# A two-block network on one core: the split of the output projections' input, a norm's sum and the attention's waits are moved

## The chip, the core and the metric

The kernel runs on one core of a Trainium2 chip. The metric is the device time in microseconds (us) of one execution. The engines are named as in the profile: PE is TensorE (PEld its weight loads), DVE is VectorE, ACT is ScalarE, POOL is GpSimd, and SP issues most of the DMAs.

## What is computed

The input is one sequence of 512 tokens with 1024 features, in float32. It goes through two different networks, one after the other. Cut to what matters here:

```
# first block (one layer)
h = rms_norm(x) ; four branches: rwkv7, mamba2 (state space), rg-lru, retention
y_ssd = rms_norm(y_state_space, norm_w)                  # a norm of its own over the 1024 features
merged = sum over the branches m of sigmoid(h @ gate_m) * (y_m @ w_branch_m)
x = x + merged @ w_out ; x = x + conv_ffn(rms_norm(x))

# second block (two layers)
h   = rmsnorm(x) ; z = h @ w_in
o_a = nsa attention, o_b = sliding window attention with sinks
o_c = mla attention: q = rmsnorm(cq) @ w_q_up, kv = rmsnorm(ckv) @ w_kv_up, 8 heads, causal softmax
g_a, g_b, g_c = sigmoid(h @ w_branch_gate)
merged = g_a * (o_a @ w_a) + g_b * (o_b @ w_b) + g_c * (o_c @ w_c)
x = x + merged @ w_out ; x = x + ffn(rmsnorm(x)) ; x = x + gated per-layer embedding
```

## The kernel before, in words

Everything stays in SBUF with features on the partitions: an activation of 1024 features is eight tiles of 128x512. The weights stream in from HBM, one tile after the other in the order in which PE uses them.

**Products.** Each float32 product is made from three fp32r products. A number is split into a high part (a copy by ACT) and a low part (number minus high part, by DVE), and PE computes high x high, low x high and high x low (`proj`, L603, whose three matmuls are L612, L613 and L614). An output tile over 1024 input features is 8 such triples, 24 matmuls (`tile`, L617). Before each triple k PE waits for the low part of input tile k. Each weight tile is split in the same way: `whi` by ACT (L1328) and `wlo` by DVE (L2044). Weights have three raw and three split buffers; the split of weight n is ordered on ACT and DVE at the place where weight n-3 is named (`ahead`, L247), and waits for PE to be done with weight n-3. Input splits are made by ACT copies and by `split_lo` (L2050, its subtraction is L2053). `h_of` gives the wait for a low part that is made by DVE, or by POOL for every third tile; `h_of_dve` the wait for one that DVE always makes.

**Order of the work.** There is one hand-written program per engine: all work of an engine is in the order of its program, and semaphores join them. `due` gives the waits that are still needed. PE writes to a ring of 7 PSUM banks (`bank`): taking a bank means waiting for whoever read its last content.

**The four merges of the first block** (`merge`, L854, L1521, L2362). For each of 8 output tiles PE computes a gate tile g(j) and a branch tile b(j), in the order g(0), g(1), b(0), g(2), b(1), and so on. In the merge of the state space branch (m = 0) the norm of that branch is applied late: ACT squares the 8 tiles (L1550), DVE adds them up (L2372), PE sums over the partitions with two float32 matmuls against ones (`total`, L1021, L1026), ACT takes the square root (L1338) and DVE the reciprocal (L2378) `MR`, by which the gates are multiplied. PE issues that sum right after b(0).

**Each layer of the second block** runs `z_proj`, `nsa`, `mla`, `branches`, the output projection (`out_proj` on ACT and DVE, `residual` on PE), `ffn` and `ple`. The two layers use different buffers: `Hx[0]` (HH, HL) and `Hx[1]` (HBh, HBl) hold the split normalized input of layer 0 and of layer 1.

- `attend` (L1162, L1860, L2893) interleaves the heads of an attention: a "first" step computes scores on PE (L1173), their maximum on DVE (L2901) and the exponential on ACT (L1868); a "second" step transposes (L1183); a "third" step multiplies by the values (L1192), with side work in between. `needs` of a job lists what the score step waits for, `vneeds` what the value step waits for.
- `mla`: PE computes q tiles and k tiles, ACT copies them out into per-head tiles QALL and KALL (L1928, L1929), two heads to a tile; DVE rotates part of q (`rope`, tile 4 for heads 0 to 3, tile 5 for heads 4 to 7). The 4 value tiles (L1269 to L1271) are side work of the first heads, and ACT copies them out into CV. Every score step waits for all of rope, all of k; every value step for all 4 tiles of CV.
- `branches` (L1279, L1966, L3027): for j in 0..7 and m in 0..2 PE computes a gate tile (24 matmuls) and a branch tile (12 matmuls). DVE multiplies the gate tile by the norm (L3051), ACT takes the sigmoid (L1978), DVE multiplies by the branch tile (L3038) and adds into the merged tile (L3043), which lies in MG in layer 0 and MGB in layer 1.
- `out_proj`: when all of `branches` is done, ACT copies the 8 merged tiles to `mp2` high parts (L1986); DVE makes the low parts of tiles 0, 1, 3, 4, 6 and 7, POOL those of 2 and 5 (`third_lo`, L3122). PE's output projection then uses them tile by tile.

What ACT and DVE do at the end of `branches` and after it, cut to its core:

```
# ACT, branches, for each j and m (n = 3 j + m)
hi(st, "g", j, m)                                  # splits one weight
wait gr(n) ; ACTV(tmp2[n % 4], tmp2[n % 4], ACT.Sigmoid)
hi(st, "b", j, m)
# ACT, out_proj
for j in range(8):
    ACTV(mp2[j][0], Mx[l][j], ACT.Copy)
```

Of the kernel before, what the change touches and what calls it, by code (L numbers as in the profile page):

```python
# [310 lines left out]
def build(nc, T, known=None):  # L311

    with ExitStack() as ctx:
# [100 lines left out]
        Mt = tiles(MG)  # L414
# [32 lines left out]
        with ExitStack() as c1:  # L447
# [43 lines left out]
            with ExitStack() as c2:  # L491
                tmp3, ACCt, tsq = tiles(sb(c2, "tmp3", 6 * S)), sb(c2, "ACCt", S), tiles(sb(c2, "tsq", 2 * S))
                with ExitStack() as c3:
                    mp2 = pairs(c3, "mp2", 8)
                act2 = pairs(c2, "act2", 11)
                PLE = sb(c2, "ple", 2 * S)
# [15 lines left out]
        TBx, OCx = [m[0:4] for m in Mx], [m[0:4] for m in Mx]  # L512
        ZCx = [m[4:8] + [ZC] for m in Mx]
# [40 lines left out]
        def nsa_jobs(l):  # L554
            jobs = []
            for qb in range(4):
# [3 lines left out]
                common = dict(qb=qb, qs=qs, needs=[("dve", "rope", "z%d" % l, 12)],  # L560
                              vneeds=[("dve", "vt", l, 3), ("act", "zt", l, 3)],
# [14 lines left out]
        def mla_jobs(l):  # L576
            st = "la%d" % l
            needs = [("dve", "rope", st, 5), ("act", "up", st, "k", 3), ("pool", "kpe", l)]
            return [dict(qb=qb, qs=slice(128 * qb, 128 * qb + 128), needs=needs, vneeds=[("act", "cv", st, 3)], pb=pbL, pt=ptL, key=("ml", l, qb),
                         nk=128 * (qb + 1), k0=0, mask=128, extra=0, s=smL[qb % 3], q=lambda h: QH[h], k=lambda h: KH[h],  # L580
                         v=lambda h, kb: CV[:, kb, 64 * h:64 * h + 64], beside=[] if qb else [(("vp", l), 5)], then=[(("out", l, qb, "c"), 3)])
                    for qb in range(4)]
# [12 lines left out]
        def tensor_program(pe):  # L595
# [25 lines left out]

            def h_of(tag):
                return lambda k: [lo_key(tag, k)]
# [230 lines left out]
            def merge(m):  # L854
# [3 lines left out]
                for j in range(8):  # L858
                    if j < 7 and (m != 3 or j):
                        gate_tile(m, j + 1)  # L860
                    tile((st, "b", j), "w_br", (m, j), 8, yp, h_of_dve(st))
                    if m == 0 and j == 0:
                        total(LN["mn"])
# [298 lines left out]
            def attend(l, jobs, side):  # L1162
                banks = {}
                for what, *x in attention_steps(jobs):
                    if what == "begin":
                        banks[x[0]["key"]] = bank("ob", *x[0]["key"], hold=True)
                    elif what == "first":
# [3 lines left out]
                        for s in due("pe", *job["needs"]):  # L1171
                            pe.wait_ge(*s)
# [69 lines left out]
            def mla(l):  # L1242
                st = "la%d" % l
                for g in (1, 0):
                    w = W.take((st, "q", g), "w_q", (l, g), 2)
                    for j in (4, 5, 3) if g else (0, 1, 2):
                        proj(bank(st, "q", j), (st, "q", j), w, cqpx[l], h_of("cq%d" % l), 128 * (j - 3 * g))
# [5 lines left out]
                for j in range(4):  # L1253
                    proj(bank(st, "k", j), (st, "k", j), w, ckp, h_of("ck%d" % l), 128 * j)
# [54 lines left out]
            for l in range(2):  # L1309
# [4 lines left out]
                residual("wo%d" % l, "w_o2", (l,), mp2, h_of("mp%d" % l))  # L1314
# [5 lines left out]
        def scalar_program(act):  # L1320
# [200 lines left out]
            def merge(m, before):  # L1521
# [24 lines left out]
                if m == 0:  # L1546
# [7 lines left out]
                    hi(st, "b", 0)  # L1554
                    evac(("ss", "mn", 0), MR, ACT.Sqrt, ("rt", "mn"), scale=1.0 / 1024, bias=EPSC)
# [410 lines left out]
            def branches(l):  # L1966
# [5 lines left out]
                for j in range(8):  # L1972
                    for m in range(3):
                        n = 3 * j + m
                        hi(st, "g", j, m)
                        for need in due("act", ("dve", "gr", st, n)):
# [5 lines left out]
            def out_proj(l):  # L1982
                for need in due("act", *ends("br%d" % l)):
                    act.wait_ge(*need)
                for j in range(8):
                    ACTV(mp2[j][0], Mx[l][j], ACT.Copy).then_inc(*up("act", "hi", "mp%d" % l, j))  # L1986
# [51 lines left out]
        def vector_program(dve):  # L2038
# [988 lines left out]
            def branches(l):  # L3027
# [17 lines left out]
                for j in range(8):  # L3045
                    for m in range(3):
                        n = 3 * j + m
                        lo(st, "g", j, m)
                        for need in due("dve", ("pe", st, "g", j, m), OWN):
# [7 lines left out]
            def out_proj(l):  # L3057
                for j in range(8):
                    if j % 3 != 2:
                        split_lo(Mx[l][j], mp2[j], ("act", "hi", "mp%d" % l, j), lo_key("mp%d" % l, j))  # L3060
# [55 lines left out]
        def gpsimd_program(pool):  # L3116
# [62 lines left out]
            for l in range(2):  # L3179
# [12 lines left out]
                third_lo("mp%d" % l, Mx[l], mp2)  # L3192
# [163 lines left out]
```

## Time and profile before

| | us |
|---|---|
| three runs | 3991.91, 3993.53, 3997.42 |
| median of the three | 3993.53 |
| the profiled execution | 3995.15 |
| span of the profile (first to last instruction) | 3993.3 |
| mean granted TensorE clock in the profile | 0.977 of full |

The page of the profile gives for each engine its busy time and its share of the span: PE 3773.1 (94%), DVE 2163.7 (54%), ACT 1497.0 (37%), POOL 104.9 (3%). How to read the views used below: the list of waits names who sat idle, on which line and tile, who released it, and for how long in total, how often, and the longest. A line of the timeline is: start, duration, engine, line and operation, output tile <- input tiles, shapes, count, and in brackets the idle time before it and who ended it. The windows view gives the busy time of engines in a stretch and the granted TensorE clock as a share of full speed.

### The profile page before, as it was taken

To read this page: it belongs to the slowest core of one execution; us is meant where nothing else is said; L and a number is where in the kernel's file an instruction comes from. 1 tells how busy PE (TensorE), PEld (TensorE's weight loads), DVE (VectorE), ACT (ScalarE), POOL (GpSimd) and SP (SyncE) were. 2 spreads that over 40 slices of the span, in tenths; PEclk is the share of its full clock that TensorE was granted. 3 is DMA by queue.
4 is the path that set the end of the run, shared out by engine and by line. 5 is a ranking of instruction groups with operands and counts; after the bars stand their busy time and mean duration, and the time that the engine had idled before them with its cause. 6 is when DMAs were issued, how large, how long until landed. Compare 5 with 4: busy or idle time off the path is not lost.

```text
span 3993.3 us, 52039 instructions
## 1 busy us (share of the span) xinstructions
PE 3773.1 (94%) x22082; PEld 3043.1 (76%) x22082; DVE 2163.7 (54%) x3219; ACT 1497.0 (37%) x2555; POOL 104.9 (3%) x132
## 2 busy tenths in 40 slices
PE   8888899799999999999999999999998999999998
PEld 6678588676876777877777887888777778878886
DVE  6844635656443566467565445434565554454345
ACT  5733324135322344343355323323434453232233
POOL 0022000100000000000001000000000010000000
PEclk9999999899999999999999999999999999999999
DMA  3100123022231222323200132232232002322322
GB/s 138 58 3 3 54 85 106 16 74 79 101 113 51 79 89 80 101 88 104 86 1 17 64 97 96 93 101 88 94 102 65 1 17 85 98 94 88 102 88 81
DMA packets 90956, 297.52 MB, mean 75 GB/s; under 512 B 10083, under 2 KB 12643, under 8 KB 90212
## 3 DMA queue, kind: packets, MB, share of 16 engines
q1 hardware_dynamic: 88848, 286.50, 21.8%
q10 hardware_dynamic: 1876, 7.71, 0.5%
q8 instruction: 173, 2.83, 0.3%
q14 instruction: 59, 0.48, 0.0%
HBM read 292.07 MB, written 2.10 MB: 74 GB/s over the span
## 4 chain that ended last, share of the span: by engine, by line
PE 81%; DVE 12%; ACT 5%; issue 1%; POOL 1%; DMA 0%; SPq 0%; DVEq 0%; ACTq 0%; POOLq 0%
PE ps L612 20%; PE ps L614 20%; PE ps L613 20%; PE ps L1173 3%; PE ps L1192 3%; DVE wlo L2044 2%; ACT whi L1328 2%; PE ps L1183 2%; DVE ftm L2060 1%; PE ps L754 1%; PE ps L638 1%; PE ps L747 1%; PE ps L759 1%; PE ps L640 1%; PE ps L639 1%
## 5 line engine op out<-in xcount | busy, mean ns | idle before, releaser
L2044 DVE TENSOR_TENSOR wlo<-wraw,whi 128x1024 fp32r<-128x1024 f32 (+5 forms) x603 | 664.0, 1103 | 1293.3 <-ACT whi L1328 1287.7
L1328 ACT ACTIVATE whi<-wraw 128x1024 fp32r<-128x1024 f32 (+5 forms) x603 | 578.1, 959 | 1302.7 <-PE ps L614 1220.0
L612 PE MATMUL ps<-HH,whi 128*128 128x512 f32 x1816 | 722.7, 398 | 9.2 <-DVE HL L2623 4.7
L614 PE MATMUL ps<-HH,wlo 128*128 128x512 f32 x1816 | 709.6, 391 | 0.0
L613 PE MATMUL ps<-HL,whi 128*128 128x512 f32 x1816 | 709.6, 391 | 0.0
L612 PEld LDWEIGHTS ps<-HH,whi 128*128 128x128 f32 x1816 | 343.0, 189 | 91.5 <-DVE HL L2623 8.1
L613 PEld LDWEIGHTS ps<-HL,whi 128*128 128x128 f32 x1816 | 342.8, 189 | 77.1 <-issue 6.3
L614 PEld LDWEIGHTS ps<-HH,wlo 128*128 128x128 f32 x1816 | 342.4, 189 | 72.4
L612 PE MATMUL ps<-HBh,whi 128*128 128x512 f32 x752 | 298.8, 397 | 6.8 <-DVE HBl L2623 6.3
L613 PE MATMUL ps<-HBl,whi 128*128 128x512 f32 x752 | 294.2, 391 | 0.0
L614 PE MATMUL ps<-HBh,wlo 128*128 128x512 f32 x752 | 294.2, 391 | 0.0
L612 PEld LDWEIGHTS ps<-HBh,whi 128*128 128x128 f32 x752 | 142.1, 189 | 41.0 <-DVE HBl L2623 8.8
L613 PEld LDWEIGHTS ps<-HBl,whi 128*128 128x128 f32 x752 | 142.1, 189 | 31.5 <-issue 2.0
L614 PEld LDWEIGHTS ps<-HBh,wlo 128*128 128x128 f32 x752 | 141.9, 189 | 30.3
L1173 PE MATMUL ps<-KPALL,ZT 128*128 128x256 f32 (+3 forms) x384 | 141.7, 455 | 22.7 <-DVE VT L2889 7.8
L612 PE MATMUL ps<-act2h,whi 128*128 128x512 f32 x384 | 152.4, 397 | 0.0
L613 PE MATMUL ps<-act2l,whi 128*128 128x512 f32 x384 | 152.2, 396 | 0.0
L614 PE MATMUL ps<-act2h,wlo 128*128 128x512 f32 x384 | 152.2, 396 | 0.0
L2901 DVE TENSOR_REDUCE sm<-ps 128x1 f32<-128x256 f32 (+3 forms) x192 | 87.1, 455 | 102.9 <-PE ps L1175 101.7
L612 PE MATMUL ps<-yph,whi 128*128 128x512 f32 x256 | 101.0, 394 | 3.5 <-DVE ypl L2053 3.5
L613 PE MATMUL ps<-ypl,whi 128*128 128x512 f32 x256 | 100.3, 392 | 0.0
L614 PE MATMUL ps<-yph,wlo 128*128 128x512 f32 x256 | 100.2, 391 | 0.0
(636 smaller groups left out, 6464.1 us busy)
## 6 DMA issues: line engine op xcount, KB each, us to landing
wraw<-in_w_ff SPq DMA_DIRECT2D x88, 512.0 KB, 3.5
wraw<-in_w_bg SPq DMA_DIRECT2D x48, 512.0 KB, 3.5
wraw<-in_ffn_up SPq DMA_DIRECT2D x44, 512.0 KB, 3.2
wraw<-in_w_z SPq DMA_DIRECT2D x36, 512.0 KB, 3.2
wraw<-in_w_gate SPq DMA_DIRECT2D x32, 512.0 KB, 3.2
wraw<-in_w_br SPq DMA_DIRECT2D x32, 512.0 KB, 3.2
wraw<-in_w_rw SPq DMA_DIRECT2D x26, 512.0 KB, 3.3
wraw<-in_w_mam SPq DMA_DIRECT2D x24, 512.0 KB, 3.2
```

What stands on the lines that cost most here:

```text
L612: MM(b[0:m, :], hi[:, k, c0:c0 + m], x[0], start=(start and k == 0), stop=False)
L613: MM(b[0:m, :], hi[:, k, c0:c0 + m], x[1], start=False, stop=False)
L614: ins = MM(b[0:m, :], lo[:, k, c0:c0 + m], x[0], start=False, stop=(stop and k == n - 1))
L638: MM(b[:, 0:cols], x[0][:, cs], hi[:, k, 0:cols], start=first, stop=False)
L639: MM(b[:, 0:cols], x[1][:, cs], hi[:, k, 0:cols], start=False, stop=False)
L640: ins = MM(b[:, 0:cols], x[0][:, cs], lo[:, k, 0:cols], start=False, stop=end)
L1173: MM(b[:, 0:nk], job["q"](h)[:, qs], job["k"](h)[:, k0:k0 + nk], start=True, stop=False)
L1183: ins = TR(b[:, 128 * kb:128 * kb + 128], job["pb"][i % 3][:, 128 * kb:128 * kb + 128], C("ident"))
L1192: ins = MM(ob[:, 64 * h:64 * h + 64], job["pt"][i % 3][:, 128 * kb:128 * kb + 128], job["v"](h, kb), start=(kb == 0), stop=(kb == nkb - 1))
L1328: ACTV(W.pair_of(n)[0], W.raw_of(n), ACT.Copy).then_inc(*up("act", "whi", n))
L2044: TT(l, W.raw_of(n), h.bitcast(F32), SUB).then_inc(*up("dve", "wlo", n))
L2901: RED(s[:, h:h + 1], PS.of("sc", *key)[:, 0:job["nk"]], AXX, ALU.max, negate=True).then_inc(*(up("dve") if x else up("dve", "mx", *key)))
```

## The change

It has three parts.

1. **Output projections of the second block.** The buffer `mp2` goes; the split merged tiles are written to the other layer's buffers (`mp2x = [Hx[1], Hx[0]]`). In `branches`, at output tile j >= 1, ACT copies merged tile j-1 after the weight split of gate (j, 1), and DVE makes its low part after the weight split of gate (j, 2). Only tile 7 is left for `out_proj`. POOL makes none of them.
2. **State space sum.** PE issues it after g(2), before b(1), where it came after b(0); ACT's weight split that belongs to g(2) is put ahead of the square root.
3. **Attention waits.** The score step of MLA waits for the rope tile, q tile and k tile of its own head, the value step for the value tiles up to its own token block; the value steps of the other attentions also name only their own token block. `h_of` goes; the two uses in `mla` named DVE for tiles 0 and 1 already.

```
@@ buffers
-                with ExitStack() as c3:
-                    mp2 = pairs(c3, "mp2", 8)
+        mp2x = [Hx[1], Hx[0]]
@@ nsa_jobs
-                common = dict(qb=qb, qs=qs, needs=[("dve", "rope", "z%d" % l, 12)],
-                              vneeds=[("dve", "vt", l, 3), ("act", "zt", l, 3)],
+                common = dict(qb=qb, qs=qs, needs=lambda h: [("dve", "rope", "z%d" % l, 12)],
+                              vneeds=[("dve", "vt", l, qb), ("act", "zt", l, qb)],
@@ mla_jobs
-            needs = [("dve", "rope", st, 5), ("act", "up", st, "k", 3), ("pool", "kpe", l)]
+            def needs(h):
+                return [("dve", "rope", st, 4 + h // 4), ("act", "up", st, "q", h // 2), ("act", "up", st, "k", h // 2),
+                        ("pool", "kpe", l)]
-            ... vneeds=[("act", "cv", st, 3)] ...
+            ... vneeds=[("act", "cv", st, qb)] ...
@@ PE, merge
+                    if m == 0 and j == 1:
+                        total(LN["mn"])
                     tile((st, "b", j), "w_br", (m, j), 8, yp, h_of_dve(st))
-                    if m == 0 and j == 0:
-                        total(LN["mn"])
@@ PE, attend
-                        for s in due("pe", *job["needs"]):
+                        for s in due("pe", *job["needs"](h)):
@@ PE, program
-                residual("wo%d" % l, "w_o2", (l,), mp2, h_of("mp%d" % l))
+                residual("wo%d" % l, "w_o2", (l,), mp2x[l], h_of_dve("mp%d" % l))
@@ ACT, merge, m == 0
                     hi(st, "b", 0)
+                    hi(st, "g", 2)
                     evac(("ss", "mn", 0), MR, ACT.Sqrt, ("rt", "mn"), scale=1.0 / 1024, bias=EPSC)
@@ ACT, branches
                         hi(st, "g", j, m)
+                        if j and m == 1:
+                            for need in due("act", ("dve", "mt", st, 3 * j - 1)):
+                                act.wait_ge(*need)
+                            ACTV(mp2x[l][j - 1][0], Mx[l][j - 1], ACT.Copy).then_inc(*up("act", "hi", "mp%d" % l, j - 1))
@@ ACT, out_proj
-                for need in due("act", *ends("br%d" % l)):
-                    act.wait_ge(*need)
-                for j in range(8):
-                    ACTV(mp2[j][0], Mx[l][j], ACT.Copy).then_inc(*up("act", "hi", "mp%d" % l, j))
+                for need in due("act", ("dve", "mt", "br%d" % l, 23)):
+                    act.wait_ge(*need)
+                ACTV(mp2x[l][7][0], Mx[l][7], ACT.Copy).then_inc(*up("act", "hi", "mp%d" % l, 7))
@@ DVE, branches
                         lo(st, "g", j, m)
+                        if j and m == 2:
+                            split_lo(Mt[j - 1], mp2x[l][j - 1], ("act", "hi", "mp%d" % l, j - 1), ("dve", "lo", "mp%d" % l, j - 1))
@@ DVE, out_proj
-                for j in range(8):
-                    if j % 3 != 2:
-                        split_lo(Mx[l][j], mp2[j], ("act", "hi", "mp%d" % l, j), lo_key("mp%d" % l, j))
+                split_lo(Mx[l][7], mp2x[l][7], ("act", "hi", "mp%d" % l, 7), ("dve", "lo", "mp%d" % l, 7))
@@ POOL
-                third_lo("mp%d" % l, Mx[l], mp2)
```

## Rows read from the trace of the kernel before

**Rows 1.** PE's waits: line, releaser, total us, times, longest us.

```profile
PE ps L612 <- DVE mp2l L2053: 12.8, 2, 6.4
...
PE ps L1173 <- DVE VT L2889: 7.8, 2, 3.9
...
PE ps L1026 <- DVE msq L2372: 5.1, 1, 5.1
...
PE ps L1192 <- ACT CV L1338: 2.8, 2, 1.4
```

**Rows 2.** Windows, most of layer 0's branches: us, PE, PEld, DVE, ACT, POOL, clock, DMA.

```profile
2205.00:2421.00 216.00, 214.43 (x974) 175.37 (x973) 102.08 (x133) 68.70 (x105) 0.00 (x0) 0.99 0.27 87
```

**Rows 3.** Timeline of PE around the state space sum.

```profile
821.85 0.39 PE L614 MATMUL ps<-yph,wlo 128*128 128x512 f32 x1
827.38 2.08 PE L1026 MATMUL ps<-msq,CT 128*128 128x512 f32 x2 [5.14 <-DVE msq L2372]
...
835.33 0.39 PE L612 MATMUL ps<-yph,whi 128*128 128x512 f32 x1
```

**Rows 4.** Timeline of PE: such a sum at full clock, at another norm.

```profile
2480.77 1.02 PE L1026 MATMUL ps<-ACCt,CT 128*128 128x512 f32 x2
```

**Rows 5.** Timeline of DVE around the state space sum.

```profile
824.24 3.08 DVE L2372 TENSOR_TENSOR msq<-msq 128x512 f32<-128x512 f32 x4
...
830.22 3.35 DVE L2378 RECIPROCAL MR<-MR 128x512 f32<-128x512 f32 x1 [1.62 <-ACT MR L1338]
```

**Rows 6.** Timeline of ACT there.

```profile
827.36 1.28 ACT L1338 ACT_TABLE_LOAD   x1
```

**Rows 7.** Timeline of PE at layer 0's output projection.

```profile
2419.89 0.40 PE L614 MATMUL ps<-oph,wlo 128*128 128x512 f32 x1
...
2426.68 0.77 PE L612 MATMUL ps<-mp2h,whi 128*128 128x512 f32 x1 [6.39 <-DVE mp2l L2053]
...
2434.53 0.40 PE L612 MATMUL ps<-mp2h,whi 128*128 128x512 f32 x1
```

**Rows 8.** Timeline of DVE at the same place.

```profile
2424.39 0.69 DVE L3043 TENSOR_TENSOR MG<-MG,tmp 128x512 f32<-128x512 f32 x1
2425.84 1.29 DVE L2053 TENSOR_TENSOR mp2l<-MG,mp2h 128x512 fp32r<-128x512 f32 x2 [0.75 <-ACT mp2h L1986]
```

**Rows 9.** Timeline of ACT at the same place.

```profile
2411.51 0.63 ACT L1978 ACTIVATE tmp<-tmp 128x512 f32<-128x512 f32 x1 [1.56 <-DVE tmp L3051]
...
2425.18 4.27 ACT L1986 ACTIVATE mp2h<-MG 128x512 fp32r<-128x512 f32 x8 [2.87 <-DVE MG L3043]
```

**Rows 10.** Windows of 1 us, PE alone: length, busy, granted clock, DMA.

```profile
803.00:804.00 1.00, 0.00 (x0) 1.00 0.00 0
...
2141.00:2142.00 1.00, 0.00 (x0) 0.65 0.00 0
```

**Rows 11.** Timeline of PE: start of layer 0's MLA; last line of layer 1's.

```profile
2162.91 0.46 PE L1173 MATMUL ps<-KALL,QALL 128*128 128x128 f32 x2 [1.85 <-ACT KALL L1929]
...
2172.01 0.43 PE L1192 MATMUL ps<-CV,ptl 128*128 128x64 f32 x2 [1.41 <-ACT CV L1338]
...
2174.91 0.33 PE L1183 MATMUL ps<-CT,tmp 128*128 128x128 f32 x1 [0.90 <-ACT tmp L1868]
...
3241.20 0.46 PE L1173 MATMUL ps<-KALL,QALL 128*128 128x128 f32 x2 [1.84 <-DVE wlo L2044]
```

**Rows 12.** Timeline of DVE: start of layer 0's MLA, then of layer 1's.

```profile
2163.95 0.28 DVE L2901 TENSOR_REDUCE sml<-ps 128x1 f32<-128x128 f32 x1
...
3238.83 2.36 DVE L2044 TENSOR_TENSOR wlo<-wraw,whi 128x1024 fp32r<-128x1024 f32 x2
```

**Rows 13.** Timeline of ACT in layer 0's MLA.

```profile
2171.84 1.06 ACT L1328 ACTIVATE whi<-wraw 128x1024 fp32r<-128x1024 f32 x1
```

**Rows 14.** Timeline of PE, the first scores of layer 0's NSA.

```profile
1978.69 0.80 PE L1173 MATMUL ps<-KPALL,ZT 128*128 128x128 f32 x2 [3.90 <-DVE VT L2889]
```

**Rows 15.** Timeline of DVE there.

```profile
1978.15 2.26 DVE L2889 TENSOR_SCALAR VT<-ps,RTC 128x256 f32<-128x256 f32 x4
```

More of the change, by code:

```diff
@@ L577, in mla_jobs @@
             st = "la%d" % l
-            needs = [("dve", "rope", st, 5), ("act", "up", st, "k", 3), ("pool", "kpe", l)]
-            return [dict(qb=qb, qs=slice(128 * qb, 128 * qb + 128), needs=needs, vneeds=[("act", "cv", st, 3)], pb=pbL, pt=ptL, key=("ml", l, qb),
+            def needs(h):
+                return [("dve", "rope", st, 4 + h // 4), ("act", "up", st, "q", h // 2), ("act", "up", st, "k", h // 2),
+                        ("pool", "kpe", l)]
+            return [dict(qb=qb, qs=slice(128 * qb, 128 * qb + 128), needs=needs, vneeds=[("act", "cv", st, qb)], pb=pbL, pt=ptL, key=("ml", l, qb),
                          nk=128 * (qb + 1), k0=0, mask=128, extra=0, s=smL[qb % 3], q=lambda h: QH[h], k=lambda h: KH[h],
@@ L620, in tile @@
                 here("pe", "w", w)
-            def h_of(tag):
-                return lambda k: [lo_key(tag, k)]
             def proj_tok(tag, name, g0, lhs, hk, cols, idx=(), beside=iter(())):
@@ L1246, in mla @@
                     for j in (4, 5, 3) if g else (0, 1, 2):
-                        proj(bank(st, "q", j), (st, "q", j), w, cqpx[l], h_of("cq%d" % l), 128 * (j - 3 * g))
+                        proj(bank(st, "q", j), (st, "q", j), w, cqpx[l], h_of_dve("cq%d" % l), 128 * (j - 3 * g))
                     here("pe", "w", w)
@@ L1253, in mla @@
                 for j in range(4):
-                    proj(bank(st, "k", j), (st, "k", j), w, ckp, h_of("ck%d" % l), 128 * j)
+                    proj(bank(st, "k", j), (st, "k", j), w, ckp, h_of_dve("ck%d" % l), 128 * j)
                 here("pe", "w", w)
```

## The prediction

> **What bounds the kernel now.** I read the list of PE's waits first, because PE is busy for nearly the whole span: what the change can give is bounded by what PE idles. Four entries touch the change [rows 1]: the low parts of the merged tiles (two waits of 6.4 us, one per layer), the first scores behind VT (two of 3.9), the squares of the state space norm (one of 5.1) and the copies of the MLA values (two of 1.4). The four come to 28.5 us, 0.7% of the span, so no outcome is large. Then I read whether PE has slack where new work is put: in layer 0's branches it is busy for 214.43 of 216 us, DVE for 102 and ACT for 69 [rows 2]. PE sets the pace there, 216 us for 974 recorded matmuls, 0.22 us each; so 24 matmuls take 5.3 us, 12 take 2.7. Last I read the timelines engine by engine around each wait, to see what is late next once it goes. Times below are positions in one profiled execution of 3995.15 us (span 3993.3); the median of the runs is 3993.53, 1.6 lower.
>
> **State space sum.** The last matmul of b(0) starts at 821.85, the sum at 827.38, b(1) at 835.33 [rows 3]; between the last two lies g(2). The squares are summed at 824.24 + 3.08 = 827.32 [rows 5], by ACT and DVE work that doesn't depend on PE's order. In the new order g(2) runs from 822.1 to 827.4, and the sum follows with next to no wait. Its two matmuls took 1.02 us at another norm [rows 4], against 2.08 here after the wait [rows 3]. So b(1) starts at 828.4: a gain of 6.9 us, 5.1 of idling and the rest from matmuls that ran slowly after it.
>
> What is late next: the split of b(2)'s weight now comes ahead of the root on ACT, and behind the end of g(2). On ACT: split from about 827.9, 1.06 long (a split of this size [rows 13]), to 829.0; table load 1.28 [rows 6] to 830.3; root about 0.63 (an ACT pass over 128x512 [rows 9]) to 830.9. On DVE: reciprocal 3.35 [rows 5] to 834.3; three passes of 0.69 [rows 8] to 836.4; b(2)'s low part, half of a pair of 2.36 [rows 12], to 837.6. PE wants it after b(1) and g(3), at 828.4 + 10.6 = 839.0. It is in time by 1.4 us. If that cover went, each us of delay beyond it is lost once; I take 6.9, and keep 5.1 as the lower end and 6.9 as the upper.
>
> The table load's row says 1.28 us. The Trainium skill (page "ScalarE: Activation LUTs", section "What ACT_TABLE_LOAD costs") counts 2.66 us for a switch, with a drain. By that the weight would come at 839.0, just as PE wants it; the sum would be the same within 0.1 us, but without any margin.
>
> **Output projection, per layer.** Before: the last branch matmul starts at 2419.89, the first of the projection at 2426.68, its second tile at 2434.53 [rows 7]. That first tile took 7.85 us where 24 matmuls should take 5.3: 2.5 us lost to slow matmuls after the idling.
> After: merged tiles 0 to 6 are split long before, so PE goes on at 2420.1 and does 7 triples until 2420.1 + 21 x 0.22 = 2424.8. Triple 7 waits for: the last addition, before at 2424.39 + 0.69 [rows 8]. It comes 0.69 later, since DVE must now make tile 6's low part ahead of the last gate product: 2425.8. The ACT copy lies between that addition's end and the first low part, 0.76 us before [rows 8]; low part 0.69; PE took it 0.15 after its end (2425.84 + 0.69 against 2426.68 [rows 7, 8]). So triple 7 starts at 2427.3, and the second tile at 2428.0. PE idles 2.5 us instead of 6.4, at another place. Gain 6.5 us, for two layers 13.0. Bounds per layer: 9.1 if triple 7 had no wait (second tile at 2425.4), 4.0 if the new idling brought the whole slow stretch of 2.5 again.
> POOL's two low parts go to DVE; nobody waits for POOL afterwards, so this costs the two DVE passes alone.
> **In the branches** 7 ACT copies and 7 DVE low parts per layer are new. The ACT copy (4.27 / 8, about 0.55 us [rows 9]) stands ahead of a sigmoid before which ACT idled 1.56 us, waiting for DVE [rows 9]: it fits in there. DVE's 0.69 delays one sigmoid per j by as much; nothing on PE waits for a sigmoid before its banks come round, and the next weights are split three ahead. I cost them at nothing; if the cover were gone, 14 x (0.55 + 0.69) = 17.4 us.
> The new wait on ACT, for the previous j's last addition, has the whole weight split stream behind it. But ACT has by then passed DVE's gate product of (j, 0), which DVE makes after that addition. It costs nothing.
>
> **MLA.** In layer 0 the first score waited 1.85 us for the last copy of k [rows 11]. It needs only the first tile of k now, so it can follow the projection at 2161.1. The value tiles beside it need a weight part that DVE makes just then. In layer 1 that part is ready at 3238.83 + 1.2 = 3240.0 [rows 12], and the first value tile began some 0.3 after 3241.20 [rows 11], so it moves up by 1.4 only. The first maximum stays where it is, at 2163.95 [rows 12], behind a weight part that waits for ACT after all of k. The exponential of head 0 is then there at about 2164.7, and PE arrives at 2161.1 + 12 x 0.22 + three scores of 0.3 = 2164.7: no new wait.
> The value step's wait of 1.41 at 2172.01 goes as well [rows 11]. But its end is not what is late next: the weight split on ACT at 2171.84 [rows 13] and its low part on DVE stand ahead of the maximum of head 5, whose transposition PE awaited at 2174.91 [rows 11]. That chain moves up only by what its start moved up. So 1.41 + 0.90 of idling become one wait of 2.3, and the gain is 1.8 in layer 0 and 1.4 in layer 1: 3.2. Ends: 0, and 2 x (1.85 + 1.41 + 0.90) = 8.3.
> **The other attentions** gain nothing. The first score started at 1978.69 [rows 14], when the first quarter of DVE's VT pass ended (1978.15 + about 0.5 [rows 15]): that is PE waiting for a bank, not for the value wait that is changed. Value steps come after all of VT is done.
>
> **The clock.** Four waits of about 2.4 us are left or made. In the idle us from 803 the granted clock stayed at full (2.4 GHz); in the one from 2141 it fell to 0.65 on average, on its way to half (1.2 GHz) [rows 10]; PE did nothing in either. So each may or may not bring a slow stretch: nothing, or up to 2.5 us. I take half of it in the projections (1.25 each) and 0.5 each in MLA, where PE has other waits: 3.5 in all.
> The Trainium skill (page "TensorE: Matmul & The Clock Gate", Part 1) says the monitor runs freely and doesn't start with the kernel, so the same code may fare differently from run to run. No single row can show that; it would leave my sum where it is and make the spread of runs its own.
>
> **The sum.** 6.9 + 13.0 + 3.2 - 3.5 = 19.6 us. From the profiled execution that is 3975.5; against the median 3973.9, so 3974.
>
> **The rivals.**
> (a) No slow stretch at any of the four: 23.1 gained, 3970. The us from 803 speaks for it, that from 2141 against. 18%.
> (b) A slow stretch at all four: 23.1 - 10.0 = 13.1, 3980. 14%.
> (c) The change doesn't do what it says outside the projections: a bank or a weight part holds PE in the sum and in MLA as VT's bank does. Only 13.0 less 2.5: 3983. 8%.
> (d) The copies in the branches are not hidden, 17.4 given back: 3991. PE's share of the branches is against it. 5%.
> (e) Slower: ACT's wait at (j, 1). If the addition came later than I read from the programs, ACT's weight splits would stop there, and PE with them from the point where the delay is over its lead of about two tiles, 8 us. Each of 14 places would cost a part of a gate and branch pair; with 4 us each, 56 - 19.6 = 36 more: 4030. It decides from 1.4 us per place. 3%.
> My forecast has the remaining 52%, with 3970 to 3978 as its own range.
>
> **How the numbers follow.** 0.2% is 8 us, about what measurements of this kernel can tell from no change: faster ends at 3985.5. Forecast, (a), (b) and (c) are faster, 92%; (d) is within, 5%; (e) slower, 3%. The range reaches over (a), (b) and (c) with the bounds of the sum: 3967 to 3983, leaving out (d), (e) and the ends of the small terms.
>
> **What would show it.** In the new profile: no wait for msq and b(1) near 828.4; a wait of about 2.5 us on the last low part in the projections, in place of 6.4; no wait for KALL or CV, but one of about 2.3 before a transposition in MLA; VT's 3.9 unchanged; branches as long as before, 216 us, with DVE at about 107. Wrong would be: branches longer, PE waiting for a weight's low part in the merge, or idling of 6 us still ahead of the projections.

## The result, and the profile after

| | us |
|---|---|
| after, four runs | 3971.71, 3972.72, 3975.65, 3976.21; median 3974.18 |
| before, four runs beside them | 3991.91 to 3997.42; median 3994.53 |
| ratio after to before | 0.9947, interval 0.9934 to 0.9960 (21 us less, 16 to 26) |
| profiled execution of after, its span | 3971.71, 3969.9 |

The changed kernel is faster by about 0.5%, as forecast, and the predicted 3974 is the median. The line numbers of the changed file are a little higher: the three matmuls of a product are L616 to L618, the sum is L1027, the scores, transposition and value step of the attention L1174, L1184 and L1193.

The list of PE's waits, in the new trace (line, releaser, total us, times, longest us):

```profile
PE ps L1174 <- DVE VT L2894: 7.8, 2, 3.9
...
PE ps L1184 <- ACT tmp L1870: 4.1, 2, 2.1
...
PE ps L616 <- DVE HL L2058: 3.6, 2, 2.1
...
PE ps L616 <- DVE HBl L2058: 2.1, 1, 2.1
```

Against [rows 1]: the two waits of 6.4 on merged low parts became one of 2.1 per layer (HBl in layer 0; in layer 1 it is the 2.1 in HL's line, whose other wait stands elsewhere). The squares' 5.1 and the value step's 1.4 are gone, and a wait of 2.1 per layer on an exponential is new. VT's 3.9 stands as it was.

**The state space sum.** PE:

```profile
830.61 0.39 PE L618 MATMUL ps<-HH,wlo 128*128 128x512 f32 x1
830.84 1.02 PE L1027 MATMUL ps<-msq,CT 128*128 128x512 f32 x2
831.29 0.79 PE L616 MATMUL ps<-yph,whi 128*128 128x512 f32 x1
...
837.18 0.39 PE L616 MATMUL ps<-HH,whi 128*128 128x512 f32 x1
```

DVE and ACT at the same place:

```profile
827.55 3.08 DVE L2377 TENSOR_TENSOR msq<-msq 128x512 f32<-128x512 f32 x4
...
834.19 3.35 DVE L2383 RECIPROCAL MR<-MR 128x512 f32<-128x512 f32 x1 [2.27 <-ACT MR L1339]
...
839.64 1.22 DVE L2049 TENSOR_TENSOR wlo<-wraw,whi 128x1024 fp32r<-128x1024 f32 x1
```

```profile
831.10 1.06 ACT L1329 ACTIVATE whi<-wraw 128x1024 fp32r<-128x1024 f32 x1 [0.43 <-PE ps L618]
832.17 1.28 ACT L1339 ACT_TABLE_LOAD   x1
833.47 0.69 ACT L1339 ACTIVATE MR<-ps,DP 128x512 f32<-128x512 f32 x1
```

The sum follows g(2)'s last matmul without a wait and takes 1.02 us, as at the other norm [rows 4], where it took 2.08 behind the idling [rows 3]. This execution reached the place 3.3 us later than the old one, because of slow matmuls far ahead of the edit: the squares end at 827.55 + 3.08 = 830.63, not at 827.32. Matched matmul by matmul (each start in the old trace against the start of the same matmul in the new one), the old trace is 3.3 us ahead of the new one before the sum and 3.6 us behind it after b(1) began: 6.9 us gained. The chain behind it (weight split, table load, root, reciprocal, b(2)'s low part) ends at 839.64 + 1.22 = 840.9, and b(2) starts at about 837.18 + 24 x 0.227 = 842.6, so the weight is in time by 1.7 us.

**The output projection of layer 0.** PE, from its first matmul to its second tile:

```profile
2413.14 0.39 PE L616 MATMUL ps<-HBh,whi 128*128 128x512 f32 x1
...
2417.69 0.39 PE L618 MATMUL ps<-HBh,wlo 128*128 128x512 f32 x1
2420.15 0.50 PE L616 MATMUL ps<-HBh,whi 128*128 128x512 f32 x1 [2.07 <-DVE HBl L2058]
...
2420.96 0.54 PE L616 MATMUL ps<-HBh,whi 128*128 128x512 f32 x1
```

DVE and ACT, which make what triple 7 waits for:

```profile
2418.01 0.69 DVE L3048 TENSOR_TENSOR MG<-MG,tmp 128x512 f32<-128x512 f32 x1
2419.40 0.69 DVE L2058 TENSOR_TENSOR HBl<-MG,HBh 128x512 fp32r<-128x512 f32 x1 [0.69 <-ACT HBh L1991]
```

```profile
2404.52 0.63 ACT L1984 ACTIVATE tmp<-tmp 128x512 f32<-128x512 f32 x1 [1.03 <-DVE tmp L3058]
...
2418.74 0.63 ACT L1991 ACTIVATE HBh<-MG 128x512 fp32r<-128x512 f32 x1 [2.81 <-DVE MG L3048]
```

PE goes from the branches straight into the projection and does seven triples. Then it waits for the chain of the last merged tile: addition until 2418.70, copy until 2419.37, low part until 2420.09. The idle time is 2.07 where the old kernel had 6.39 [rows 7].

There is a second gain here, which the prediction has no term for. These are the starts of the third and fourth tile of the projection, before and after, all at full granted clock:

```profile
2440.15 0.40 PE L612 MATMUL ps<-mp2h,whi 128*128 128x512 f32 x1
...
2445.78 0.40 PE L612 MATMUL ps<-mp2h,whi 128*128 128x512 f32 x1
```

```profile
2433.48 0.39 PE L616 MATMUL ps<-HBh,whi 128*128 128x512 f32 x1
...
2438.92 0.39 PE L616 MATMUL ps<-HBh,whi 128*128 128x512 f32 x1
```

A tile of 24 matmuls took 5.63 us with its input in `mp2` and 5.44 us with it in HBh and HBl, that is 0.234 and 0.227 us a matmul. It is 0.234 in both layers of all three traces that have `mp2` (before, p2, p3) and 0.227 in both layers of the ten others. Behind the second tile this adds up to 1.2 us per layer. Why the old buffers were read more slowly is not shown by any run.

The windows view (us, PE, PEld, DVE, ACT, POOL busy, granted clock, DMA), for most of layer 0's branches and for the first us behind the new gaps of both projections:

```profile
2200.00:2416.00 216.00, 215.15 (x985) 176.43 (x984) 105.92 (x141) 72.74 (x113) 0.00 (x0) 1.00 0.28 89
...
2421.00:2425.00 4.00, 4.00 (x12) 3.13 (x11) 1.82 (x2) 1.89 (x3) 0.00 (x0) 0.57 0.09 23
...
3489.00:3493.00 4.00, 4.00 (x12) 3.14 (x11) 1.82 (x2) 1.90 (x3) 0.00 (x0) 0.57 0.10 24
```

DVE has 4 us more to do in 216 us than in [rows 2] and ACT 4 too, and PE is as busy as before. (Both windows begin some 15 us ahead of the branches, in MLA; matched by matmul, the branches themselves took the same time within 0.05 us, but for a slow stretch at their start in the old trace.) Behind each gap PE ran at a mean of 0.57 of the full clock, that is at 1.2 GHz for most of the four us: it did the work of 4 x 0.57 = 2.3 us in them, and 1.7 us were lost.

**MLA in layer 0.** PE:

```profile
2157.39 0.38 PE L1174 MATMUL ps<-KALL,QALL 128*128 128x128 f32 x2
...
2165.08 0.33 PE L1193 MATMUL ps<-CV,ptl 128*128 128x64 f32 x2
...
2166.66 0.33 PE L1184 MATMUL ps<-CT,tmp 128*128 128x128 f32 x1 [0.29 <-ACT CV L1339]
...
2169.56 0.33 PE L1184 MATMUL ps<-CT,tmp 128*128 128x128 f32 x1 [2.07 <-ACT tmp L1870]
```

The first score (2157.39) and the first value step (2165.08) have no wait. Head 5's transposition has one of 2.07 us in place of the 1.41 and 0.90 of [rows 11]. It starts at 2169.56 where it started at 2174.91: 5.35 earlier, against 3.52 ahead of the MLA. So 1.8 us gained.

### The profile page after: what moved, and what is told of

Read it like the earlier page. It is cut to its first block, busy times and chain, and to the rows that moved or that the text cites. A ratio compares the mean times of both kernels' runs of the same rounds, so it can differ in the third digit from the quotient of the medians.

```text
span 3969.9 us, 52034 instructions
## 1 busy us (share of the span) xinstructions
PE 3766.9 (95%) x22082; PEld 3041.9 (77%) x22082; DVE 2161.4 (54%) x3223; ACT 1496.3 (38%) x2555; POOL 99.8 (3%) x128
## 4 chain that ended last, share of the span: by engine, by line
PE 82%; DVE 12%; ACT 5%; issue 1%; POOL 0%; DMA 0%; SPq 0%; DVEq 0%; ACTq 0%; POOLq 0%
PE ps L616 21%; PE ps L618 20%; PE ps L617 20%; PE ps L1174 3%; PE ps L1193 3%; DVE wlo L2049 2%; ACT whi L1329 2%; PE ps L1184 2%; DVE ftm L2065 2%; PE ps L755 1%; PE ps L748 1%; PE ps L760 1%; PE ps L639 1%; PE ps L641 1%; PE ps L640 1%
## 5 line engine op out<-in xcount | busy, mean ns | idle before, releaser
L616 PE MATMUL ps<-HH,whi 128*128 128x512 f32 x1880 | 746.6, 397 | 11.2 <-DVE HL L2628 4.7
L618 PE MATMUL ps<-HH,wlo 128*128 128x512 f32 x1880 | 734.6, 391 | 0.0
L617 PE MATMUL ps<-HL,whi 128*128 128x512 f32 x1880 | 734.3, 391 | 0.0
L616 PEld LDWEIGHTS ps<-HH,whi 128*128 128x128 f32 x1880 | 354.7, 189 | 95.8 <-DVE HL L2628 8.1
L617 PEld LDWEIGHTS ps<-HL,whi 128*128 128x128 f32 x1880 | 354.7, 189 | 79.1 <-issue 5.8
L618 PEld LDWEIGHTS ps<-HH,wlo 128*128 128x128 f32 x1880 | 354.3, 188 | 75.1
L616 PE MATMUL ps<-HBh,whi 128*128 128x512 f32 x816 | 323.7, 397 | 8.9 <-DVE HBl L2628 6.3
L617 PE MATMUL ps<-HBl,whi 128*128 128x512 f32 x816 | 319.1, 391 | 0.0
L618 PE MATMUL ps<-HBh,wlo 128*128 128x512 f32 x816 | 319.0, 391 | 0.0
L616 PEld LDWEIGHTS ps<-HBh,whi 128*128 128x128 f32 x816 | 153.9, 189 | 46.2 <-DVE HBl L2628 8.9
L617 PEld LDWEIGHTS ps<-HBl,whi 128*128 128x128 f32 x816 | 154.0, 189 | 33.7 <-issue 2.0
L618 PEld LDWEIGHTS ps<-HBh,wlo 128*128 128x128 f32 x816 | 153.9, 189 | 32.9
L1174 PE MATMUL ps<-KPALL,ZT 128*128 128x256 f32 (+3 forms) x384 | 140.6, 451 | 22.7 <-DVE VT L2894 7.8
L616 PE MATMUL ps<-act2h,whi 128*128 128x512 f32 x384 | 152.5, 397 | 0.0
L618 PE MATMUL ps<-act2h,wlo 128*128 128x512 f32 x384 | 152.2, 396 | 0.0
L616 PE MATMUL ps<-yph,whi 128*128 128x512 f32 x256 | 101.4, 396 | 3.5 <-DVE ypl L2058 3.5
L618 PE MATMUL ps<-yph,wlo 128*128 128x512 f32 x256 | 100.2, 391 | 0.0
```

Of the source, the lines that this page charges most:

```text
L616: MM(b[0:m, :], hi[:, k, c0:c0 + m], x[0], start=(start and k == 0), stop=False)
L617: MM(b[0:m, :], hi[:, k, c0:c0 + m], x[1], start=False, stop=False)
L618: ins = MM(b[0:m, :], lo[:, k, c0:c0 + m], x[0], start=False, stop=(stop and k == n - 1))
L1174: MM(b[:, 0:nk], job["q"](h)[:, qs], job["k"](h)[:, k0:k0 + nk], start=True, stop=False)
```

## The experiments

Eleven runs were made, of eight edited kernels and of the changed one again. Ratios are to the kernel before, on the same chip; its median was 3994.0 us in the first two groups (p1, p2, p3, last_first; both_later, wait_first, copies3, after_again) and 3994.1 in the last (later_only, last_first2, both_later2). Edits are to the changed kernel.

**1. The parts alone: p1, p2, p3.** p1 keeps the new output projections and undoes the other two parts. p2 is the kernel before with the sum moved alone:

```
# p2, on the kernel before
                     hi(st, "b", 0)
+                    hi(st, "g", 2)
...
+                    if m == 0 and j == 1:
+                        total(LN["mn"])
                     tile((st, "b", j), "w_br", (m, j), 8, yp, h_of_dve(st))
-                    if m == 0 and j == 0:
-                        total(LN["mn"])
```

p3 is the kernel before with the attention waits alone:

```
# p3, on the kernel before
-                         vneeds=[("dve", "vt", l, 3), ("act", "zt", l, 3)]
+                         vneeds=[("dve", "vt", l, qb), ("act", "zt", l, qb)]
...
-            needs = [("dve", "rope", st, 5), ("act", "up", st, "k", 3), ("pool", "kpe", l)]
+            def needs(h):
+                return [("dve", "rope", st, 4 + h // 4), ("act", "up", st, "q", h // 2), ("act", "up", st, "k", h // 2),
+                        ("pool", "kpe", l)]
...
-            vneeds=[("act", "cv", st, 3)]
+            vneeds=[("act", "cv", st, qb)]
```

> Only the output projections' part (input split tile by tile into the other layer's buffers). My theory: it carries the largest share. Each layer's wait on the low parts shrinks from 6.4 us to about 2.1, stands ahead of the eighth triple and not the first, and some of the slow matmuls after it go: 5 to 6.5 us per layer, 10 to 13 in all, ratio about 0.9970. The squares' wait of 5.1 us and MLA's waits of 1.85 and 1.41 stay. Rival (the parts help each other, for instance because the whole shortening comes from fewer slow stretches of TensorE's clock): less than 6 us here, and the three parts alone don't add up to the 20 us of the whole.

> Only the state space sum's part. My theory: 6.9 us (b(1) comes 7 us earlier against the squares), ratio about 0.9983; the wait for the squares is gone, and no wait for a weight's low part takes its place, though ACT's root now stands behind one more weight split. Rival (a weight comes late in its place): a wait of PE on a weight's low part within three tiles of the sum, and a gain under 5.5 us.

> Only the attention waits' part. My theory: 1.8 us in layer 0 and 1.4 in layer 1, up to 2 us less if a slow stretch follows the longer wait that remains: 1 to 3 us in all, ratio about 0.9993, near the edge of what five rounds can tell. In the profile: the waits for KALL (1.85) and CV (1.41) are gone, one of about 2.1 stands ahead of the transposition of head 5, VT's two waits of 3.9 are unchanged. Rival (the value wait was worth its 1.41 us too): the transposition of head 5 comes 3.2 us earlier against the projection of k, and 6 us in all.

| | median us | ratio, interval | gain by the ratio | the prediction's term |
|---|---|---|---|---|
| p1, projections | 3978.97 (5 runs) | 0.9967, 0.9955 to 0.9980 | 13.2 | 13.0 - 2.5 = 10.5 |
| p2, sum | 3987.88 (11 runs) | 0.9982, 0.9973 to 0.9991 | 7.2 | 6.9 |
| p3, attention waits | 3991.29 (11 runs) | 0.9996, 0.9987 to 1.0005 | 1.6 | 3.2 - 1.0 = 2.2 |

The three gains add up to 22.0, and the whole gives 21.2 by its ratio: the parts neither help nor hinder each other beyond what can be told. p1's 13.2 is nearer to what its trace gives with the faster reading of the input, 6.3 us in layer 0 and 6.4 in layer 1, than to the 10.5 of the prediction. Each removes its own waits and no other. From the list of PE's waits of p1 (the old waits of the two parts that it lacks are there again):

```profile
PE ps L1026 <- DVE msq L2375: 5.1, 1, 5.1
...
PE ps L1173 <- ACT KALL L1929: 3.7, 2, 1.8
...
PE ps L1192 <- ACT CV L1338: 2.8, 2, 1.4
...
PE ps L615 <- DVE HBl L2056: 2.1, 1, 2.1
```

and of p3, where the attention's own waits changed and nothing else:

```profile
PE ps L615 <- DVE mp2l L2056: 12.8, 2, 6.4
...
PE ps L1029 <- DVE msq L2375: 5.1, 1, 5.1
...
PE ps L1186 <- ACT tmp L1871: 4.1, 2, 2.1
```

p3's interval takes in no effect at all; that its waits moved is shown by the trace, that it gains is not shown by its times alone.

**2. What the new wait of the projections hangs on: last_first.** At b(7, 2) DVE made the low part of a later weight (1.2 us) ahead of the last product with a branch tile and the last addition. Here these two come first. (The expectation calls it the low part of the last branch weight; by the rule of three ahead it is that of the projection's third weight, and it is 128x1024 where a branch weight is 128x512.)

```
+                        if n == 23:
+                            gated(n)
                         lo(st, "b", j, m)
-                        gated(n)
+                        if n < 23:
+                            gated(n)
```

> The whole change, and in the branches DVE makes the last gate product and the last addition (n = 23) ahead of the low part of the last branch weight, where it stood behind it. My theory of the remaining 2.1 us: on DVE a weight's low part of 1.23 us, itself behind ACT's high part of 1.04, stands ahead of the last gate product, though sigmoid and branch tile were there 2.3 us before. With the order turned, the last low part comes about 2.3 us earlier, the wait of 2.1 us ahead of the eighth triple goes to under 0.3 in both layers, and with it the slow stretch behind it: 2.1 to 3.6 us per layer, 4 to 7 against the changed kernel, ratio to before about 0.9934. Rival (the wait is set by PE's own end and the chain of product, addition, copy and low part alone): it stays at 1.5 us or more.

Measured: 3968.38 (5 runs), ratio 0.9932 (0.9920 to 0.9944). It ran once more in the last group, beside the kernels of experiment 5:

> last_first once more, on the chip of both_later2. My theory: 3964 to 3969. It sets the distance to both_later2 on one chip.

3959.53 (4 runs), ratio 0.9914 (0.9901 to 0.9928). All nine runs together have a median of 3963.0, against 3972.7 for the nine runs of the changed kernel (the first four and the five of experiment 4): 10 us less, from an edit that adds and removes no instruction. The second occasion came out below the 3964 to 3969 that was expected of it. The timeline of DVE:

```profile
2414.30 0.69 DVE L3048 TENSOR_TENSOR MG<-MG,tmp 128x512 f32<-128x512 f32 x1
2414.91 1.22 DVE L2049 TENSOR_TENSOR wlo<-wraw,whi 128x1024 fp32r<-128x1024 f32 x1
2416.05 0.69 DVE L2058 TENSOR_TENSOR HBl<-MG,HBh 128x512 fp32r<-128x512 f32 x1
```

and the clock where the changed kernel had its slow us:

```profile
2417.00:2425.00 8.00, 8.00 (x36) 6.61 (x36) 2.44 (x3) 3.46 (x4) 0.00 (x0) 1.00 0.42 132
```

The low part of tile 7 is there at 2416.7, and PE starts triple 7 at 2416.78, some 0.3 us later than at its own pace. With the gap of 2.07 went the 1.7 us of slow matmuls behind it: up to 3.8 us per layer. Matched by matmul, the new execution gains 3.6 us over each projection, 7.1 in all; the rest of the 10 us between the medians is not placed.

**3. Is there a price in the branches? wait_first and copies3.** The first puts ACT's wait and copy ahead of the weight split of gate (j, 0), so that ACT stands there until DVE's addition, with the whole stream of weight splits behind it:

```
-                        hi(st, "g", j, m)
-                        if j and m == 1:
+                        if not (j and m == 0):
+                            hi(st, "g", j, m)
+                        if j and m == 0:
                             for need in due("act", ("dve", "mt", st, 3 * j - 1)):
                                 act.wait_ge(*need)
                             ACTV(mp2x[l][j - 1][0], Mx[l][j - 1], ACT.Copy)...
+                            hi(st, "g", j, m)
```

> Edit: the changed kernel, with ACT's wait for the last addition of a merged tile and its copy put ahead of the weight split of gate (j, 0), instead of behind that of gate (j, 1). ACT now stands at each of the 14 places until DVE's addition, with all weight splits behind it. My theory (the splits run about two tiles, 8 us, ahead of PE, so a delay of a few us on ACT is taken from the lead): the branches stay within 1 us of 216 us per layer, the total within 2 us of the changed kernel, 3972 to 3976. Rival (the prediction's slower case: the lead is small, each of 14 places costs 2 to 4 us): 28 to 56 us more, 4000 to 4030, with waits of PE on low parts of branch weights.

The second makes each of the 14 copies three times:

```
                         if j and m == 1:
                             ...
+                            for again in range(2):
+                                ACTV(mp2x[l][j - 1][0], Mx[l][j - 1], ACT.Copy).then_inc(*up("act"))
+                                for need in due("act", OWN):
+                                    act.wait_ge(*need)
                             ACTV(mp2x[l][j - 1][0], Mx[l][j - 1], ACT.Copy)...
```

> Edit: the changed kernel, with each of the 14 ACT copies of merged tiles made three times, one after the other (28 copies more of about 0.6 us each, some 17 to 20 us with the waits between them). The part of the computation is the same. My theory (ACT's copy is hidden, PE has its banks and weights long before): branches as long as before, total within 2 us, 3972 to 3976. Rival (the copy is only just hidden, ACT's idle of 1.0 us ahead of the sigmoid is all there is): what goes beyond 1.0 us at each place shows on PE, up to 14 x 0.5 = 7 us more.

Measured: wait_first 3970.53 (4 runs), ratio 0.9943 (0.9928 to 0.9958); copies3 3971.10 (4 runs), ratio 0.9941 (0.9928 to 0.9955). Both are the changed kernel's time, 1 us or so under the 3972 to 3976 that was expected. ACT does wait in wait_first, and the next split follows it:

```profile
2390.77 0.63 ACT L1982 ACTIVATE HBh<-MG 128x512 fp32r<-128x512 f32 x1 [2.81 <-DVE MG L3050]
2391.85 0.63 ACT L1329 ACTIVATE whi<-wraw 128x512 fp32r<-128x512 f32 x1 [0.45 <-PE ps L618]
```

In copies3 the copies use up the idle time ahead of the sigmoid (1.03 us with one copy):

```profile
2403.52 1.28 ACT L1982 ACTIVATE HBh<-MG 128x512 fp32r<-128x512 f32 x2
2404.83 0.63 ACT L1985 ACTIVATE HBh<-MG 128x512 fp32r<-128x512 f32 x1
2405.37 0.61 ACT L1988 ACTIVATE tmp<-tmp 128x512 f32<-128x512 f32 x1
```

and PE does not notice. Its busy time in copies3, in the window used above:

```profile
2200.00:2416.00 216.00, 215.15 (x986) 176.49 (x986) 106.50 (x141) 80.16 (x127) 0.00 (x0) 1.00 0.28 89
```

Matched by matmul against the changed kernel, neither execution loses or gains as much as 0.05 us over the branches of either layer. So ACT has 1.3 us to spare at each place beyond the copy, and can also stand for 2.81. DVE's low parts were not doubled; that they are hidden rests on the branches of the changed kernel, which are as long as the old ones.

**4. The changed kernel again: after_again.**

> The changed kernel as it is, beside the other three on one chip: 3974 within 3 us. It shows how much of what differs between its first profile and the others is the execution's own: if the slow matmul stretches after the short gaps at 2421 and 3489 us are a matter of the phase of the clock alone, some of them stand elsewhere or are missing; if they follow from the gaps, they stand again at the same places.

3972.64 (5 runs), ratio 0.9947 (0.9935 to 0.9960), the same ratio on another occasion. The windows of its trace:

```profile
2171.00:2175.00 4.00, 4.00 (x19) 3.13 (x19) 1.53 (x5) 1.61 (x7) 0.00 (x0) 0.57 0.15 52
2424.00:2428.00 4.00, 4.00 (x12) 3.16 (x11) 1.82 (x2) 2.11 (x3) 0.00 (x0) 0.57 0.20 40
3245.00:3250.00 5.00, 4.88 (x39) 4.16 (x39) 2.91 (x9) 3.65 (x15) 0.00 (x0) 1.00 0.01 3
3492.00:3496.00 4.00, 4.00 (x12) 3.14 (x11) 1.82 (x2) 1.40 (x2) 0.00 (x0) 0.57 0.00 0
```

Behind the projections' gaps (second and fourth line) the clock fell again. Behind MLA's gap it fell in layer 0 and not in layer 1; in the first trace of the changed kernel it was the other way round:

```profile
2150.00:2200.00 50.00, 47.48 (x302) 37.70 (x301) 28.96 (x60) 33.50 (x96) 0.00 (x0) 1.00 0.10 32
3236.00:3241.00 5.00, 5.00 (x25) 3.98 (x26) 1.76 (x5) 2.41 (x11) 0.00 (x0) 0.66 0.20 52
```

Over all traces: six executions have the gap of 2.07 in both projections (the changed kernel's two, p1, wait_first, copies3, later_only), and the clock fell behind all twelve gaps. The four executions without it (last_first and both_later, twice each) show no slow stretch there.

MLA is another matter. Every trace has a slow stretch ahead of its scores, at about 2141 and 3220 us in the old one; the count here is of those behind it. The traces have 14 layers with the gap of 2.07 us in MLA (the changed kernel, p3, last_first, wait_first and copies3) and 12 without it (before, p1, p2, both_later twice, later_only). In the 14, six slow stretches follow the gap, and MLA ends without one. In the 12, seven stand at MLA's end, each at the same short wait of 0.85 us, and an eighth (p1, layer 1) at its start. The kernel before, at the end of layer 1's MLA:

```profile
3298.06 0.44 PE L1239 MATMUL ps<-CT,oab 128*128 128x128 f32 x2 [0.85 <-DVE oab L2949]
```

```profile
3296.00:3304.00 8.00, 7.14 (x32) 5.96 (x32) 4.30 (x7) 5.05 (x13) 0.00 (x0) 0.79 0.00 0
```

So the layers with the gap had no more slow stretches than those without it, 6 in 14 against 8 in 12; the stretch behind the gap is not shown to be a cost that the change added.

**5. What the new wait in MLA hangs on: both_later, later_only.** On top of last_first, both_later moves a weight split, on ACT and DVE, from value step 4 to step 11. later_only is that move alone. (The expectation calls the weight the output projection's. What is ordered under the value weight's name is the split of the weight three further on, that of gate (0, 1) of the branches; the edit moves that one.)

```
-    beside=[] if qb else [(("vp", l), 5)]
+    beside=[] if qb else [(("vp", l), 12)]
@@ ACT, side work of the value tiles
-                    elif step:
+                    elif 0 < step < 5:
                         evac((st, "v", step - 1), ...)
-                        if step == 4:
-                            hi(st, "v")
+                    elif step == 11:
+                        hi(st, "v")
@@ DVE
-  lo(st, "v") if name[0] == "vp" and step == 4 else None
+  lo(st, "v") if name[0] == "vp" and step == 11 else None
```

> Edit: last_first, and in MLA the split of the output projection's weight goes from value step 4 of head 0's row to step 11, on ACT and DVE, the value tiles' own output step with it. My theory (the wait of 2.07 us ahead of the transposition behind head 5's exponential in layer 0, and its like in layer 1, comes from that split and its low part standing ahead of a maximum, 1.1 + 1.2 us): the two waits go or fall below 0.5 us, 1.5 to 2 us per layer, so 3 to 4 us less than last_first: 3964 to 3965. Rival 1 (the wait comes from the evacuations of the value tiles, not from the split): the waits stay at 2, the time is last_first's within 1. Rival 2 (the split is late at its new place): a new wait on the weight's low part ahead of step 12's matmuls, and no gain.

> Edit: the changed kernel with the move of MLA's weight split alone (value step 4 to step 11), without the move of the last gate product. In both_later the two waits of 2.07 us went down to 0.3, yet its median lay 11 us under last_first's, which ran on another chip, where the traces give 1.8 us per layer and one slow stretch of 3.4 us (1.7 us of loss) per execution. My theory (11 is 5 from those, and the rest spread of the runs): 5 us less than the changed kernel, 3967 to 3970. Rival (the move is worth about 11 by a way that I don't see): 3961 to 3963.

> both_later once more, on the chip of last_first2. My theory: 5 us under last_first2, 3959 to 3963. Rival: 11 us under it, 3954 to 3958.

The wait went down to 0.3, as the list of PE's waits in layer 0's MLA shows for both_later:

```profile
PE ps L1184 <- ACT tmp L1870: 0.3, 1, 0.3
```

Times: both_later 3957.52 (4 runs), ratio 0.9911 (0.9898 to 0.9925); again 3961.02 (4 runs), 0.9916 (0.9903 to 0.9930); later_only 3968.37 (5 runs), 0.9935 (0.9922 to 0.9949). Alone the move gives 4.3 us against the nine runs of the changed kernel (3972.7), near the 2 x 1.8 of the waits. On top of last_first it gives 3.3 over all runs (3959.7 of eight against 3963.0 of nine), but in the one group in which both ran together both_later was 1.5 us slower. The first distance of 11 us was mostly spread: last_first itself ran at 3968.4 on one occasion and at 3959.5 on another. Neither the 3964 to 3965 expected of both_later nor the 5 or 11 us expected between the two in the last group came. So the wait's cause is shown; the move's worth on top of last_first is not settled. Both_later is the fastest version by its pooled median, 0.9% under the kernel before.

The slow stretches in MLA don't hang on this gap. Without it both_later's clock still fell once, at MLA's end as in the kernel before (experiment 4):

```profile
3274.00:3279.00 5.00, 4.56 (x15) 3.80 (x16) 2.38 (x5) 3.45 (x10) 0.00 (x0) 0.66 0.00 0
```

## Why the prediction was right, point by point

Locally, by matching the matmuls of the two traces (old start less new start, ahead of each place and behind it):

| step | predicted | shown |
|---|---|---|
| sum of the squares | 6.9 | 6.9 |
| projection, layer 0 and layer 1 | 5.25 each (6.5 less 1.25 for the clock) | 6.2 and 6.4: 5.1 and 5.2 up to the second tile and the slow matmuls behind it, 1.2 from the faster reading in the tiles after |
| MLA, layer 0 and layer 1 | 1.8 and 1.4, less 0.5 each | 1.8 and -0.4 |
| branches | 0 | 0.0 in both |
| other attentions | 0 | 0 |
| sum | 19.6 | 20.9 |

The two profiled executions differ by 23.4 us. What is left, 2.5, is -3.3 from slow matmuls of the new execution early on, +4.9 from three slow stretches of the old one at about 2220, 3114 and 3298 us that the new one lacks, and 0.9 of small steps. The first and the last of the three stand at the end of MLA; whether the change moved them or chance did is open (experiment 4). The medians differ by 20.3.

- **Sum:** right in size and in what is late next. The weight's margin was put at 1.4 us and was 1.7. The table load took 1.28 us, and the root began 833.47 - 832.16 = 1.31 us after the split. Of the rest of the 2.66 us, a drain, that the Trainium skill counts (page "ScalarE: Activation LUTs", section "What ACT_TABLE_LOAD costs") nothing shows here; the measurement decides, and the margin stood.
- **Projections:** the new gap was put at 2.5 us, and is 2.07: seven triples took 0.3 us longer than by 0.22 a matmul, and the chain of addition, copy and low part was 0.15 shorter. Two things were read wrong. The first is the clock's term. I took half a slow stretch per gap, of 2.5 us; there was a whole one each time, of 1.7 us. 1.7 less the 0.4 of the shorter gap is the 1.25 that I had, so two errors cancelled. The second is the one price of 0.22 us for every matmul. It was an average over a window that began with MLA's short matmuls; at full clock the old projection took 5.63 us a tile, not 5.3, and the new one 5.44. The 1.2 us per layer that this gives was in no term.
- **MLA:** the wait on the values did turn into one on head 5's exponential, of 2.07 instead of 2.3, and the gain in layer 0 is the forecast one. In layer 1 the gain of 1.4 was spent on a slow stretch of 1.7, which in the next execution stood in layer 0. Over all traces it is 6 stretches behind 14 such gaps, 0.7 us each; I had 0.5. But the prediction charged them as new, and layers without the gap had as many; the old execution's at 3298 offsets the one in layer 1.
- **Branches and ACT's wait:** nothing, and experiment 3 shows that there was room.
- **Luck:** the total of 3974 is closer than its terms. The clock's share in the projections was right by two errors, and 2.1 us too little there stood against 0.8 too much in MLA and against what the executions add of their own.
- **The free-running monitor** of the Trainium skill (page "TensorE: Matmul & The Clock Gate", Part 1): in MLA the traces agree, since the same gap in the same kernel brought 1.2 GHz once and full clock once. In the projections chance played no part that twelve gaps could show.

**The rivals.** (a), no slow stretch, is refuted by the windows. (b), all four slow, holds for the projections, but in MLA for 6 gaps in 14. (c) falls with p2 and with the waits of p3. (d) and (e) fall with copies3 and wait_first, (d) for ACT's copies alone, and for DVE's low parts with the unchanged length of the branches.

What I did not see: the new gap of the projection, which I had worked out to 0.4 us, was there for the taking by the order of two DVE steps, and so was the one in MLA.

## What to carry to other kernels

Where the last input of a product is late, let all other inputs be ready first; the wait shrinks to the chain behind the last one. Then read that chain: a split for a later weight that stands ahead of it in an engine's program delays the whole chain, and moving it was free here (7 us by the matched traces, 10 by the medians, for an edit of a few lines). Count a PE gap of 2 us ahead of dense float32 work as nearly 4 on this kernel, since the clock fell behind each of twelve such gaps. And where one buffer is exchanged for another, compare PE's time for the same tile in both: it was 3% here, at the same clock.

## What was not expected of the hardware

- The same fp32r matmul of 512 columns took 0.234 us reading `mp2` and 0.227 reading HBh or HH, in every trace and at full granted clock. Why is open.
- How surely the clock falls depends on the place. Behind the gap of 2.07 us in the projections it fell 12 times in 12; behind the gap of 2.07 us in MLA 6 times in 14, in the traces of seven executions: in six of them in just one of the two layers, in the seventh (p3's) in none. Why is open: what PE did before differs (dense matmuls of 512 columns there, short ones with small waits here), and so does the time since the last slow stretch, and no run here parts the two. That layers without this gap have a slow stretch at MLA's end, behind 0.85 us of idling, more often than not (7 in 12) shows that the length of the gap alone doesn't decide.
- The spread of the runs differs between kernels that differ in two DVE steps: nine runs of the changed kernel lie within 6.0 us, nine of last_first within 13.0 (on two occasions each). No run tells why. Differences of a few us need both kernels in one group, and even then several runs.
